# Bias rows of the differential attention stored once and repeated by eight transfers, and the first roots of its norm moved by one memory head

## The reference

```python
xn = rmsnorm(x, lp['norm_mix_w'])
z = xn @ lp['w_in']
rq, rk, rv, rg, dq, dk, dv, mq, ga, gb, gc = jnp.split(z, offs, axis=-1)
...
o_d = diff_attend(...)          # differential attention, bias by relative position
o_m = mem_attention(mq, mem_k, mem_v)
mixed = sigmoid(ga) * (o_r @ w_up_ret) + sigmoid(gb) * (o_d @ w_up_diff) + sigmoid(gc) * (o_m @ w_up_mem)
```

```python
o = jnp.einsum('bhqk,bkhe->bqhe', a, v)
o = rmsnorm(o, subln_w) * (1.0 - lam_init)
```

## Time and profile before

| | |
|---|---|
| median of 3 runs | 3171.03 us (3170.27 to 3171.88) |
| profiled execution | 3170.03 us, span in the trace 3168.2 us |
| PE busy | 2982.9 us, 94% |
| VectorE, ScalarE, GpSimd busy | 1833.7 (58%), 1267.2 (40%), 1028.4 us (32%) |
| mean granted TensorE clock | 0.975 |
| DMA | 698.29 MB, mean 220 GB/s |

### The profile page before, as it was taken

The page is one execution under the profiler, slowest core; times in us unless marked ns, Lnnn a source line. Parts: engine busy times, 40 slices in busy tenths (PEclk is TensorE's granted clock), DMA queues, the critical chain, the costliest instruction groups (busy, mean ns, idle before and its releaser), DMA issues. The chain is left out here.

```text
span 3168.2 us, 52281 instructions
## 1 busy us (share of the span) xinstructions
PE 2982.9 (94%) x20998; PEld 2783.5 (88%) x20998; DVE 1833.7 (58%) x2566; ACT 1267.2 (40%) x1399; POOL 1028.4 (32%) x551
## 2 busy tenths in 40 slices
PE   5899999899989867999999999999999999999997
PEld 5899999887878857999899999999998888888886
DVE  3444444365321134643658899877885577667764
ACT  4332322345533444433344443555544333333332
POOL 0000000134645430003238888877776011101000
PEclk9899999999999888999999999999999999999999
DMA  7554555475576626677758999999999788888764
GB/s 206 162 163 159 168 170 166 146 234 175 168 238 207 211 75 199 195 218 189 156 130 195 226 252 218 262 301 272 260 296 338 273 299 313 313 300 303 287 202 172
DMA packets 449140, 698.29 MB, mean 220 GB/s; under 512 B 30853, under 2 KB 345637, under 8 KB 421446
## 3 DMA queue, kind: packets, MB, share of 16 engines
q1 hardware_dynamic: 398622, 553.81, 56.8%
q10 hardware_dynamic: 41160, 75.51, 8.9%
q0 software_dynamic: 9216, 67.11, 5.6%
HBM read 627.14 MB, written 63.70 MB: 218 GB/s over the span
## 5 line engine op out<-in xcount | busy, mean ns | idle before, releaser
L2606 POOL TENSOR_TENSOR peer_uT_low<-peer_uT,peer_uT_high 128x1024 fp32r<-128x1024 f32 x256 | 615.6, 2429 | 253.8 <-ACT peer_uT_high L2633 252.9
L1040 POOL TENSOR_TENSOR gate_low<-gate_raw,gate_high 128x512 fp32r<-128x512 f32 x192 | 256.7, 1363 | 908.6 <-ACT gate_high L991 908.2
L2506 PE MATMUL banks<-x_high,peer_uT_high 128*128 128x256 f32 x2048 | 491.7, 282 | 5.1 <-ACT peer_picks_T L2665 5.1
L2507 PE MATMUL banks<-x_low,peer_uT_high 128*128 128x256 f32 x2048 | 487.7, 280 | 0.0
L2506 PEld LDWEIGHTS banks<-x_high,peer_uT_high 128*128 128x128 f32 x2048 | 385.4, 188 | 5.8 <-ACT peer_uT_high L2633 2.9
L2507 PEld LDWEIGHTS banks<-x_low,peer_uT_high 128*128 128x128 f32 x2048 | 384.7, 188 | 0.0
L247 PE MATMUL banks<-x_high,win_high 128*128 128x288 f32 (+1 forms) x1312 | 351.8, 298 | 20.4 <-DVE in_mem_kv_T L915 20.4
L248 PE MATMUL banks<-x_low,win_high 128*128 128x288 f32 (+1 forms) x1312 | 351.0, 296 | 0.0
L217 ACT ACTIVATE win_high<-win_raw 128x2048 fp32r<-128x2048 f32 x84 | 160.8, 1915 | 361.0 <-DVEq L210 342.5
L2756 DVE STREAM_TRANSPOSE peer_uT<-peer_u 128x1024 f32<-128x1024 f32 x192 | 234.2, 1229 | 84.9 <-DMA peer_u<-in_peer_u_dram 58.8
L2633 ACT ACTIVATE peer_uT_high<-peer_uT 128x1024 fp32r<-128x1024 f32 x256 | 260.7, 1055 | 54.1 <-DVE peer_uT L2756 53.5
(11 more groups left out here) (396 smaller groups left out, 6513.3 us busy)
## 6 DMA issues: line engine op xcount, KB each, us to landing
win_raw<-in_w_in_dram SPq DMA_DIRECT2D x38, 2048.0 KB, 8.1
peer_u<-in_peer_v_dram SPq DMA_DIRECT2D x64, 1024.0 KB, 5.4
peer_area<-in_peer_v_dram SPq DMA_DIRECT2D x64, 1024.0 KB, 5.9
gate_raw<-in_w_in_dram SPq DMA_DIRECT2D x96, 512.0 KB, 4.7
peer_u<-in_peer_u_dram SPq DMA_DIRECT2D x192, 256.0 KB, 5.8
peer_u<-in_peer_u_dram ACTq DMA_DIRECT2D x192, 256.0 KB, 6.6
w_raw<-in_w_up_ret_dram SPq DMA_DIRECT2D x8, 2048.0 KB, 9.9
w_raw<-in_w_out_dram SPq DMA_DIRECT2D x8, 2048.0 KB, 8.5
```

The source lines that it names most:

```text
L1040: pool.tensor_tensor(self.low[:, p % 2, c, :, :], self.raw[:, p % 4, :, c * P:(c + 1) * P], self.high[:, p % 2, c, :, :], ALU.subtract).th ...
L2506: pe.matmul(out, UH[:, c, k, :], XH[:, k, 0:DENSE], start=(k == 0), stop=False)
L2507: pe.matmul(out, UH[:, c, k, :], XL[:, k, 0:DENSE], start=False, stop=False)
L2606: pool.tensor_tensor(UL[:, m % 2, part, :], UT[:, m % 2, part, :], UH[:, m % 2, part, :], ALU.subtract).then_inc(low, 1)
```

## The change

The bias rows are stored once, 8 x 512, to a new tensor `bias_row`. Eight new transfers, one for each head, copy a row from there to `bias_rows`, 128 times each, from memory to memory (`repeat_rows`). They are issued by ScalarE behind the high parts of units 13 (three), 14 (three) and 15 (two), the first behind a wait for the store; SyncE's wait at the stage's end is now for the eight. Apart from that, the roots of the first four differential heads, which stood behind the exponentials of memory head 3, now stand at the end of memory head 2, behind `keep_pair`.

```diff
-             "bias_rows": scratch("bias_rows", (DIFF_HEADS, P, 512)),
+             "bias_row": scratch("bias_row", (DIFF_HEADS, 512)), "bias_rows": scratch("bias_rows", (DIFF_HEADS, P, 512)),
...
                 for u in range(1, 4):
                     w.split_high(act, FIRST_Z + 1, u)
+                    for h in range(3 * u - 3, min(3 * u, DIFF_HEADS)):
+                        diff.repeat_rows(act, h)
...
-        self.dram = G["S"]["bias_rows"]
+        self.row_dram, self.dram = G["S"]["bias_row"], G["S"]["bias_rows"]
...
     def store_rows(self, act):
         act.wait_ge(self.kept, after(1))
-        act.dma_start(self.dram, self.rows.unsqueeze(1).to_broadcast([DIFF_HEADS, P, 512])).then_inc(self.rows_stored, 16)
+        act.dma_start(self.row_dram, self.rows).then_inc(self.rows_stored, 16)
+
+    def repeat_rows(self, act, h):
+        if h == 0:
+            act.wait_ge(self.rows_stored, after(16))
+        act.dma_start(self.dram[h], self.row_dram[h].partition_broadcast(P)).then_inc(self.repeated, 16)
 
     def wait_scratch_free(self, sp):
-        sp.wait_ge(self.rows_stored, after(16))
+        sp.wait_ge(self.repeated, after(16 * DIFF_HEADS))
...
                         if h == 0:
                             norm.squares(act)
-                        if h == MEM_HEADS - 1:
-                            norm.roots(act, 0)
                         gates.act(act, TICKS_MEM[0])
...
                         gates.keep_pair(act)
+                        if h == MEM_HEADS - 2:
+                            norm.roots(act, 0)
```

More of the change, by code:

```diff
@@ L1089, in __init__ @@
                               ("diff_lambda_q1", "diff_lambda_k1", "diff_lambda_q2", "diff_lambda_k2"))]
-        self.dram = G["S"]["bias_rows"]
+        self.row_dram, self.dram = G["S"]["bias_row"], G["S"]["bias_rows"]
         sem = G["signals"].take
-        self.ones_row, self.loaded, self.picked, self.lam_steps, self.biased, self.kept, self.rows_stored = (sem() for _ in range(7))
+        self.ones_row, self.loaded, self.picked, self.lam_steps, self.biased, self.kept, self.rows_stored, self.repeated = (sem() for _ in range(8))
     def load(self, sp):
```

## The result

The changed kernel takes **3152.19 us** (median of 4 runs, 3151.19 to 3152.55) against 3171.23 us; ratio 0.994, 95% interval 0.9927 to 0.9954. That is 19.0 us less; the forecast was 22.7 less. Run again on two more chips, it took 3150.15 us (0.9931 [0.9918, 0.9945]) and 3149.38 us (0.9931 [0.9917, 0.9944]): 21.0 and 22.5 less than the kernel before beside it. Over all 14 executions it spreads from 3147.68 to 3152.99 us, so the same program differs from itself by more (5.3 us) than the forecast missed the first median (3.9 us).

What follows compares the result with a forecast made beforehand. TensorE, 94% busy, was taken as the bound, so only its idle or half-clock time could be gained: 20.4 + 2.5 + 0.1 + 0.8 - 1.1 = 22.7 us off 3171.0 gives 3148.3 us (forecast 3145.5 to 3150.5, range 3143.5 to 3157).

Steps and rivals of the forecast that it cites:

- Part 1, the hole: Before product 6, PE's idle time of 20.4 us vanishes once the bias store no longer delays the first `mem_T` store.
- Part 1, the clock: Product 6 ran at half clock behind the hole; without the hole it runs at full clock, gaining 2.5 us.
- nothing in the sum: Half clock behind the short wait for `x_low` may fall or not: ±1.7 us in the range, not counted.
- rival A: Repeats as heavy as the old bias packets, 0.2 to 0.37 us each: stall 4 to 14.8 us, 3151 to 3162; chance 0.13.
- Part 2, +1.1 us: Eight repeats delay the weight load for unit 16 and may stall PE: cost 1.1 us, half of a 2.1 us stall.
- if read and written bytes share the rate: For memory-to-memory repeats, packet time doubles to 0.17 us, unit 16's load lands 10.9 us later, PE stalls 2.1 us.
- a new wait of PE between 60 and 180 us: Sign that the prediction was wrong: PE idling anew in the stretch of the stores, the repeats and unit 16's load.
- The sign named for A or B: ScalarE's wait before unit 16 ended by a load instead of VectorE's queue; its length would then show either rival.
- B: Sixteen engines queue on one 2 KB memory row, stalling PE 38 us before unit 16: slower, 3185 us; chance 0.03.
- Part 3, +0.8 us: In memory head 3, moved roots start the gate split 0.8 us earlier; PE's wait shrinks from 5.62 to 4.9 us.
- C: First `mem_T` store slow for its own reason, or another wait replaces it: only 0.8 us gained, 3170; chance 0.04.
- D: Both half-clock stretches, behind `x_low` and memory head 3's wait, vanish and no stall comes: 3144 us; chance 0.10.

Runs made afterwards that it cites:

- the delay: The changed kernel with one 128x1024 memset on VectorE ahead of the scaling of the memory rows: 3152.36 us, ratio 0.9939 to the kernel before.
- the roots' own run: The kernel before with only the roots moved behind memory head 2, bias store left as it was: 3170.97 us, ratio 1.0004.
- the run from one partition: The changed kernel with each of the eight repeats reading its row from its SBUF partition instead of memory: 3212.77 us, ratio 1.0136.
- the roots where ScalarE idles: The changed kernel with logarithms before head 2's output copy and exponentials before the copy of head 3's probabilities: 3146.91 and 3144.32 us.

## Why the prediction was right, and where not

**Part 1, the hole: right, with its cause.** Both stores take 2.9 us, neither VectorE nor PE waits there, the granted clock is 1.00, and the product behind `x_low` begins at 85.01, 108.90 - 85.01 = 23.9 us earlier (forecast 23.0 with the issue; 85.36 and 85.19 in the other two profiles). Part of that was there ahead of the hole and goes with the execution: the small store is issued at 48.45 instead of 49.09, and in other profiles without the delay anywhere up to 49.49. Counted from that issue the product comes 36.6 us later in each of the three, where it came 108.90 - 49.09 = 59.8 us later before (59.3 in the roots' own run). So 22.7 to 23.3 us are the change's, and the term of 0.1 us for the shorter issue is too small to be told apart in that; ScalarE idles 0.58 instead of 1.29 us before the high part behind it. The cost per packet, 0.37 us, was measured rightly. The guess that the source would matter, "not eight SBUF partitions but memory", was right too, as the run from one partition shows.

**Part 1, the clock: the term that failed.** The 2.5 us of product 6 were gained at that place. For the stretch behind `x_low` the text put "nothing in the sum", with ±1.7 us, as for the one behind the wait of memory head 3 (-1.8 us), and it took all others as unchanged. Instead PE's busy time is 2982.8 us after 2982.9: what some stretches gave back, others took. Two that are longer in the first profile: behind `x_low`, 80 to 95 us, and 1090 to 1100 us above (0.83, where the same place of before, 1113 to 1123, has 1.00). The first, after and (second fence) before:

```profile
80.00:95.00 15.00, 13.04 (x75) 11.78 (x73) 10.01 (x11) 6.47 (x6) 0.00 (x0) 0.77 0.31 102
```

```profile
105.00:120.00 15.00, 13.04 (x78) 11.31 (x77) 10.01 (x11) 8.06 (x10) 0.00 (x0) 0.89 0.38 127
```

That is 15 x 0.12 x 2 = 3.6 us more at half clock. In the second and third profile the same 15 us have 0.89, as before, and in the second one of the roots where ScalarE idles they have 1.00. Such stretches fall differently in each execution: in three profiles of one program the busy time differs by 2.3 us, the 14 times by 5.3. So the 2.5 us that one profile shows for a half-clock stretch could not be counted on as a gain in the total.

The first median, 3152.19, lies in the stated range but outside the forecast's own 3145.5 to 3150.5, in the time that was set aside for rival A, whose stall did not come. The other two, 3150.15 and 3149.38, lie inside it. Without the 2.5 us the sum is 20.2, or 3150.8, next to the median of all 14 executions, 3150.7. That it is so close is luck in part: of the terms that remain the stall did not cost its 1.1, the 0.8 of the roots does not show, and the two errors nearly cancel.

**Idle time.** The waits that the change was to shorten lost 20.4 + 0.7 us, PE's idle time 18.4 to 20.3 in all. In the first profile 1.7 came back in PE's wait for `x_high`, 5.0 before:

```profile
PE banks L2246 <- ACT x_high L2198: 6.7, 1, 6.7
```

In the third it is 5.0 again, and with the roots unmoved it was 5.0 once and 6.7 once. That too goes with the execution, not with the change.

**Part 2, +1.1 us: too high, measured 0, 0.51 and 0 in three profiles.** The form of the step held (load late by 64 p, slack 8.8), p was 0.12 us between the bounds 0.085 and 0.37, and 7.8 is less than 8.8. The step that failed was "if read and written bytes share the rate": the packet lay below 0.17, nearer to the lower end. In the second profile the load took 19.4 us, so p was (19.4 - 10.3) / 64 = 0.14, and PE stood for 0.51, which by the prediction's own sign ("a new wait of PE between 60 and 180 us") is a small stall of the kind that it feared. The sign named for A or B, a load that ends ScalarE's wait before unit 16, was too strict: it does (7.95 us), and PE doesn't stall, since it is still at work on unit 15. Issue times were 0.5 to 1.5 us each, under the 4.4 us of idle time, as foreseen. Rivals A (repeats as heavy as the bias packets) and B (one row of memory as a hot spot) fell with this number: both needed a packet of 0.2 us or more.

**Part 3, +0.8 us: the wait right, the gain not seen.** The wait shrank from 5.62 to 4.95 (0.67), in the roots' own run to 4.94, yet that run is 1.0004 [0.9994, 1.0013] of before. 0.7 us is an eighth of the changed kernel's spread of 5.3. That the wait does not shrink by the 4.84 us of the roots was right, and the version with the roots in ScalarE's idle time takes 3.51 us more off it.

Rivals C, that the change doesn't do what it says, and D, that both half-clock stretches vanish, did not come; a stretch behind `x_low` was there in all three profiles (0.77, 0.89, 0.89).

## What to carry to other kernels

A transfer that repeats a few SBUF partitions many times ran here at 28 to 44 GB/s and held back, packet for packet, the other queue on its engines. Store the rows once and repeat them from memory, behind the transfers that something waits for, and work out the slack of the next load first. A sum made of waits held to 2 us here. Gains by the clock were not to be counted on before several executions showed them. And work that an engine must do in the way of the bottleneck belongs where that engine already waits for it, cut in two if need be.

## What the runs showed of the hardware

- A 2 KB packet cost the load behind it 0.12 to 0.14 us (16 engines, from one row in memory). It took 0.37 us on eight engines from eight SBUF partitions (44 GB/s in all), and 1.05 us on sixteen engines with one partition to a transfer (28 GB/s in all from 165 to 175 us).
- The two queues passed the same number of packets where the slow store ran (217 to 213, and 216 to 215, in 10 us).
- Issues of the transfers from one partition took up to 12.1 us each on ScalarE, six of eight above 3.6, where those from memory took 0.5 to 1.5. Why an issue lasts so long no run shows.
- The same program with the same wait of PE ahead ran at 1.2 GHz for 3.4 us more or less in one place from one execution to the next, and its times spread by 5.3 us.
